# Values projected by three split products, a block table by one-hot products, and a gate weight split later

## The chip, the cores and the metric

One core of one Trainium2 chip runs the program. The metric is device time of one execution in microseconds (us): 2423.96 as the median of 3 runs (2423.73 to 2424.24).

The core has a matrix engine (PE, with its weight loads as PEld), a vector engine (DVE), a scalar engine (ACT), GpSimd (POOL) and a queue engine (SP). Each runs its own instructions strictly in order. An instruction may wait for a semaphore, and everything behind it on its engine then waits too.

## What is computed

One layer of a backbone over 2048 latent tokens and 256 context tokens of width 1024, in float32. This is what matters of the reference:

```
h   = rmsnorm(x) * (1 + scale) + shift                     # scale, shift from silu(c) @ w_mod
z, xbc, dt, q, k, v, g_out, gk = split(h @ w_in)           # one projection
xbc = silu(conv(xbc)); gates = log_sigmoid(gk @ gk_up + bias) / 16
two scans (SSD over xbc, dt; GLA over q, k, v, gates), both directions, context first
x   = x + gate * (concat(norm(ssd) * silu(z), norm(gla) * silu(g_out)) @ w_out)
ids, w = route(h2 @ w_router)                              # top 2 of 32 experts per token
slots: each (token, expert) pair gets a place in blocks of 128 rows, one expert to a block
x   = x + gate2 * sum_over_experts(w * mlp_e(h2));  out = rmsnorm(x)
```

`v` is the 512 columns of `w_in` from `O_V`; `z` and `g_out` are 512 columns each, from `O_Z` and `O_G`.

## The kernel before, in words

The stages run one after the other, each as a block of five instruction lists, with a barrier behind each: constants and modulation, projection, chunks, mixer, slots, experts, combine.

**Projection** (`projection`, lines 350 to 782). There are nine groups of 256 tokens, the context first (`it` 0), then eight of latents. `head` normalises a group (ACT squares, L494; POOL the root, L566; DVE scales, L686), PE transposes it (`turned`, L593) and DVE modulates it into `hT` (L695). `body` has on PE five pairs of feature products (L614, 128x256, plain float32), half a slab of the modulation (L267), the small columns (L628), and then per 128 tokens `s` the value product into `pz[s]` (L636, 8 products 128x512 in float32, each of which the trace shows as two instructions), with the transposes of the **next** group between and behind them. ACT takes each pair out of PSUM (L506, L512), then waits for DVE's convolution, applies Silu (L516), and only then squares the next group (`head(*after)`). So ACT's order is: fifth pair, Silu, next group's squares. In groups 5 to 7 one piece of the `z`/`g_out` weight is split in `w_hi` (ACT L547) and `w_lo` (DVE L776). A split is x = hi + lo, both in the reduced type fp32r.

**Chunks** (`chunks`). The product of `z` and `g_out` (L1060) is made of three fp32r products hi*hi, hi*lo, lo*hi per 128 rows `k`. `KA` = 3 pieces of the weight come split from the projection; pieces 3 to 5 are loaded there but split at the start of this stage, and pieces 6 and 7 are loaded (L871) as buffers come free, and split (ACT L939, DVE L1122) behind DVE's and ACT's first chunk work. PE waits per `k` for `w_lo_done`.

**Slots** (`slots`, lines 1821 to 2028). DVE works out each pair's slot in a chain of short instructions, each waiting for the one before (`then`), POOL clears a table `slot_tok` in DRAM, waits for the slots, and scatters 32 times 128 records of 16 words (token, weight) into it by indirect DMA (L1911). DVE meanwhile makes the block plan (L2008 to L2027).

**Experts** (`experts`). POOL loads the table (L2122), copies a block's indices (L2118) and gathers its rows (L2120). PE transposes them (`turn`, L2229), ACT and DVE split them (L2168, L2295) and the weights (L2163, L2289), PE multiplies (L2236).

## Time and profile before

| | us |
|---|---|
| median of 3 runs | 2423.96 |
| the profiled execution, whole | 2428.52 |
| its span in the profile | 2426.8 |
| modulation, until the first feature product | 0 to 53.9 |
| projection | 53.9 to 604.1 |
| chunks | 604.1 to 901 |
| mixer | 901 to 1321 |
| slots | 1321 to 1404.3 |
| experts | 1404.3 to about 2384 |
| combine | to 2426.8 |

PE is busy for 2164.6 us (89% of the span), DVE 1624.7 (67%), ACT 1137.1 (47%), POOL 529.8 (22%). To read it: times are us from the span's start, matmuls are pipelined, so a busy PE is not at its peak, and the profile also gives the clock that PE was granted, as a share of full speed (1.00 is 2.4 GHz, 0.50 is 1.2 GHz). Stages follow each other through barriers, so what one stage gains or loses shifts all behind it.

### The profile page before, as it was taken

How to read it: one execution, taken by the hardware profiler on the slowest of the kernel's cores; microseconds unless marked ns; L12 is line 12 of the kernel's file. 1: busy time of each engine (PE TensorE's matmuls, PEld its weight loads, DVE VectorE, ACT ScalarE, POOL GpSimd, SP SyncE). 2: the span in 40 equal slices, each digit the busy share in tenths (PEclk: the TensorE clock that was granted, in tenths of full speed). 3: DMA queues.
4: the chain of work that ended last, by engine and by line, in shares of the span. 5: the costliest groups of instructions: out<-in, count | busy, mean ns of one | idle time of the engine just before them, and what ended most of it. 6: DMA issues, size and time to landing. Idle time of an engine off the chain costs nothing. (4 is left out here: it accounts for less than half of the span.)

```text
span 2426.8 us, 36201 instructions
## 1 busy us (share of the span) xinstructions
PE 2164.6 (89%) x11697; PEld 1709.4 (70%) x11697; DVE 1624.7 (67%) x2071; ACT 1137.1 (47%) x1469; POOL 529.8 (22%) x536
## 2 busy tenths in 40 slices
PE   4999999998999987999996059999999999999980
PEld 2777777776777766888885048878788778778760
DVE  1333333433666667777773449999999999999983
ACT  0222222222555533333331047777777777777763
POOL 1000000000000001233322423333332333333332
PEclk7999999999999996899997579999999999999995
DMA  8123334322688745899874426478988779989957
GB/s 317 66 78 108 110 117 145 128 99 85 228 291 295 277 171 191 305 311 293 291 240 113 176 54 207 115 241 275 303 253 274 233 233 356 310 293 309 374 182 293
DMA packets 204877, 530.22 MB, mean 218 GB/s; under 512 B 14929, under 2 KB 46156, under 8 KB 198252
## 3 DMA queue, kind: packets, MB, share of 16 engines
q1 hardware_dynamic: 174904, 424.71, 48.8%
q0 software_dynamic: 26224, 91.57, 15.0%
q10 hardware_dynamic: 3651, 12.65, 1.4%
q8 instruction: 61, 1.00, 0.2%
q14 instruction: 37, 0.30, 0.0%
HBM read 398.64 MB, written 130.24 MB: 218 GB/s over the span
## 5 line engine op out<-in xcount | busy, mean ns | idle before, releaser
L2163 ACT ACTIVATE w_hi_e<-w_gates 128x2048 fp32r (+1 forms) x103 | 197.7, 1920 | 237.1 <-issue 104.1
L2289 DVE TENSOR_TENSOR w_lo_e<-w_gates,w_hi_e 128x2048 fp32r<-128x2048 f32 x103 | 236.4, 2296 | 33.2 <-ACT w_hi_e L2163 33.2
L2289 DVE TENSOR_TENSOR w_lo_e<-w_ups,w_hi_e 128x2048 fp32r<-128x2048 f32 x102 | 233.5, 2289 | 37.0 <-ACT w_hi_e L2163 37.0
L2289 DVE TENSOR_TENSOR w_lo_e<-w_downs,w_hi_e 128x2048 fp32r<-128x2048 f32 x100 | 228.4, 2284 | 0.0
L2163 ACT ACTIVATE w_hi_e<-w_ups 128x2048 fp32r (+1 forms) x102 | 195.2, 1914 | 24.8 <-PE pd_e L2236 22.4
L2163 ACT ACTIVATE w_hi_e<-w_downs 128x2048 fp32r x100 | 191.1, 1911 | 1.0
L614 PE MATMUL pf<-raws,w_in_sb 128*128 128x256 f32 x800 | 177.5, 385 | 1.1 <-DVE raws L695 1.1
L2236 PE MATMUL pg_e<-w_hi_e,x_hi_e 128*128 128x512 f32 x408 | 167.7, 411 | 7.2 <-DVE w_lo_e L2289 7.2
L614 PEld LDWEIGHTS pf<-raws,w_in_sb 128*128 128x128 f32 x800 | 154.1, 193 | 23.0 <-DVE raws L695 1.5
L2141 POOL DMA_INDIRECT x_mid<-yb_e,to_e x50 | 126.9, 2538 | 190.7 <-DVE yb_e L2333 188.6
L2236 PE MATMUL pg_e<-w_lo_e,x_hi_e 128*128 128x512 f32 x408 | 162.1, 397 | 0.0
L2236 PE MATMUL pd_e<-w_hi_e,h_hi_e 128*128 128x512 f32 x400 | 162.1, 405 | 0.0
L2236 PE MATMUL pg_e<-w_hi_e,x_lo_e 128*128 128x512 f32 x408 | 161.9, 397 | 0.0
L2236 PE MATMUL pd_e<-w_hi_e,h_lo_e 128*128 128x512 f32 x400 | 157.9, 395 | 0.0
L2236 PE MATMUL pu_e<-w_hi_e,x_hi_e 128*128 128x512 f32 x400 | 157.9, 395 | 0.0
L2236 PE MATMUL pu_e<-w_hi_e,x_lo_e 128*128 128x512 f32 x400 | 157.9, 395 | 0.0
L2236 PE MATMUL pu_e<-w_lo_e,x_hi_e 128*128 128x512 f32 x400 | 157.9, 395 | 0.0
L2236 PE MATMUL pd_e<-w_lo_e,h_hi_e 128*128 128x512 f32 x400 | 157.9, 395 | 0.0
L614 PE MATMUL pf<-hT,w_in_sb 128*128 128x256 f32 x640 | 143.8, 388 | 0.0
L2118 POOL COPY idx_e<-toks_e 128x1 int32 (+1 forms) x54 | 51.5, 954 | 400.7 <-DMA x_mid<-yb_e,to_e 335.9
L614 PEld LDWEIGHTS pf<-hT,w_in_sb 128*128 128x128 f32 x640 | 124.7, 195 | 17.7
L716 DVE TENSOR_SCALAR fm<-u_raw,cols 128x256 f32<-128x256 f32 x54 | 18.2, 411 | 176.2 <-ACT u_raw L506 176.2
(420 smaller groups left out, 4708.4 us busy)
## 6 DMA issues: line engine op xcount, KB each, us to landing
w_gates<-in_w_gate_dram SPq DMA_DIRECT2D x32, 2048.0 KB, 12.1
w_ups<-in_w_up_dram SPq DMA_DIRECT2D x32, 2048.0 KB
w_downs<-in_w_down_dram SPq DMA_DIRECT2D x32, 2048.0 KB
w_mod_half<-in_w_mod_dram SPq DMA_DIRECT2D x16, 1024.0 KB, 7.0
abc_m<-a_rows SPq DMA_DIRECT2D x16, 1024.0 KB, 4.9
recs<-tok_rec SPq DMA_DIRECT2D x15, 968.0 KB, 7.8
qk_rec<-qk SPq DMA_DIRECT2D x14, 1024.0 KB, 3.9
qk<-qk_rec SPq DMA_DIRECT2D x14, 1024.0 KB
```

The lines of the kernel that those rows point to most:

```text
L614: mm = pe.matmul(pf[n % 2][:, f, :], w[:, k, c0:c0 + P], h[:, k, :], start=(k == 0), stop=(k == KT - 1))
L716: i = dve.tensor_scalar(a, b, wt, cols[:, R_CB + f:R_CB + f + 1], ALU.mult, ALU.add)
L2118: pool.tensor_copy(idx[u][:, :], toks[:, bass.ds(b, 1), 0]).then_inc(idx_ready, 1)
L2141: pool.indirect_dma_start(out=x_mid, out_offset=bass.IndirectOffsetOnAxis(ap=to[u][:, 0:1], axis=0), in_=yb[:, :], in_offset=None, compute ...
L2163: act.activation(w_hi[:, s % 3:s % 3 + 1, :], raw(part, half, place), ACT.Copy).then_inc(hi_done, 1)
L2236: mm = pe.matmul(acc[:, :], a[:, k, :], w[:, s % 3, c], start=start and n == 0, stop=stop and n == 2)
L2289: dve.tensor_tensor(w_lo[:, s % 3:s % 3 + 1, :], raw(part, half, place), w_hi[:, s % 3:s % 3 + 1, :].bitcast(F32), ALU.subtract).then_inc( ...
```

## The change

Three edits go together.

**Values.** The `v` columns leave the big weight load (`W_LEN` falls from 1800 to 1288 columns). They are loaded apart, in pieces of 256 rows, at the start of the projection, and split once, in the context group, into `wv_hi` and `wv_lo`. Each 128 tokens of `hT` are split into `x_hi` (ACT, `high`) and `x_lo` (DVE, `low`), each with one buffer. The value product becomes 24 fp32r products (`values`). That of `s` = 0 now stands on PE **ahead of the fifth feature pair**, that of `s` = 1 between the two halves of the next group's transposes. `high` of `s` = 1 stands on ACT ahead of taking out the fifth pair.

**Gates' weight.** `KA` = 0: no piece is split in the projection, three are loaded at its end, and the chunk stage splits all eight.

**Block table.** POOL's clearing and 32 scatters, and the table's load in the experts, go. DVE makes, in four rounds of 8 tiles, a one-hot of each pair's place in its block (128x1024), a one-hot of its block (128x544), and this times token and weight; PE sums them by 32 float32 products 128x136 into PSUM, and DVE copies the table to SBUF at the end of its list.

```diff
@@ -51,7 +51,7 @@
 FF = 512
 EPS = 1e-6
 MAXB = 64
-KA = 3
+KA = 0
 BIG = 1e30
 
 
...
@@ -70,7 +70,7 @@
 T_DT = T_V + GW
 T_GF = T_DT + 2 * SH
 T_LEN = T_GF + 2 * GQK
-W_LEN = O_G - O_XBC
+W_LEN = O_V - O_XBC
 
 F_TILES = 6
 
...
-            slots(nc, A, C, route, slot_tok, weights, loaded, x_mid, h_rows)
-            experts(nc, A, C, route, slot_tok, weights, loaded, h_rows, x_mid)
+            toks = ctx.enter_context(nc.sbuf_tensor("toks", [P, TAB, 2], I32))
+            slots(nc, A, C, route, toks, weights, loaded, x_mid, h_rows)
+            experts(nc, A, C, route, toks, weights, loaded, h_rows, x_mid)
         combine(nc, A, x_mid, out)
 
 
...
             for k in range(KT):
-                sp.dma_start(w_in_sb[:, k, :], A["w_in"][0][k * P:(k + 1) * P, O_XBC:O_G]).then_inc(w_in_loaded, 16)
+                sp.dma_start(w_in_sb[:, k, :], A["w_in"][0][k * P:(k + 1) * P, O_XBC:O_V]).then_inc(w_in_loaded, 16)
...
-        w_raw, w_hi, w_lo = K["w_raw"], K["w_hi"][0], K["w_lo"][0]
-        SPLIT = LAT_GROUPS - KA
+        F32R = mybir.dt.float32r
+        w_raw = K["w_raw"]
+        wv_hi, wv_lo = sb("wv_hi", [P, KT, GW], F32R), sb("wv_lo", [P, KT, GW], F32R)
+        x_hi, x_lo = sb("x_hi", [P, KT, P], F32R), sb("x_lo", [P, KT, P], F32R)
+        wv_loaded = [sem(f"wv{b}_loaded") for b in range(3)]
+        wv_hi_done, wv_lo_done, x_hi_done, x_lo_done = (sem(n) for n in ("wv_hi_done", "wv_lo_done", "x_hi_done", "x_lo_done"))
+        PAIRS = KT // 2
...
+
+            def load_v(c):
+                if c >= 3:
+                    sp.wait_ge(wv_lo_done, c - 2)
+                for n in range(2):
+                    k = 2 * c + n
+                    sp.dma_start(w_raw[c % 3][:, n, :], A["w_in"][0][k * P:(k + 1) * P, O_V:O_G]).then_inc(wv_loaded[c % 3], 16)
+            for c in range(3):
+                load_v(c)
...
                 sp.dma_start(sel_dt[ONE:ONE + 1, SH * d:SH * (d + 1)], A[f"dt_bias_{n}"]).then_inc(small_loaded, 16)
 
             sp.dma_start(slab[:, :, :], w_mod_d[EARLY][0]).then_inc(slab_loaded, 16)
+            load_v(3)
...
-                if it == SPLIT - 1:
+                if it == LAT_GROUPS - 1:
+                    sp.wait_ge(wv_lo_done, PAIRS)
                     for k in range(3):
                         load_w(k)
-                if SPLIT <= it < LAT_GROUPS:
-                    sp.wait_ge(K["w_lo_done"], it - SPLIT + 1)
-                    load_w(it - SPLIT + 3)
...
+            def high(it, buf, s):
+                if s:
+                    act.wait_ge(tok_ps, it * 2 + 1)
+                else:
+                    act.wait_ge(ht_done, it * 4 + 4)
+                    if not it == 0:
+                        act.wait_ge(tok_ps, it * 2)
+                act.activation(x_hi[:, :, :], hT[buf][:, :, s * P:(s + 1) * P], ACT.Copy).then_inc(x_hi_done, 1)
+
...
 
+                high(it, buf, 0)
+                if is_ctx:
+                    for c in range(PAIRS):
+                        act.wait_ge(wv_loaded[c % 3], 32 * (c // 3 + 1))
+                        act.activation(wv_hi[:, 2 * c:2 * c + 2, :], w_raw[c % 3], ACT.Copy).then_inc(wv_hi_done, 1)
                 for n in range(5):
+                    if n == 4:
+                        high(it, buf, 1)
                     act.wait_ge(feat_ps, it * 5 + (n + 1))
...
-                if SPLIT <= it < LAT_GROUPS:
-                    k = it - SPLIT
-                    act.wait_ge(K["w_loaded"][k % 3], 32 * (k // 3 + 1))
-                    act.activation(w_hi[:, k, :, :], w_raw[k % 3][:, :, :], ACT.Copy).then_inc(K["w_hi_done"], 1)
...
+            def values(it, s, is_ctx):
+                if s == 0 and not is_ctx:
+                    pe.wait_ge(min_done, it * 4)
+                    pe.wait_ge(abs_done, it * 4)
+                if is_ctx:
+                    pe.wait_ge(wv_lo_done, PAIRS)
+                pe.wait_ge(x_lo_done, it * 2 + s + 1)
+                for k in range(KT):
+                    for j, (a, b) in enumerate(((x_hi, wv_hi), (x_hi, wv_lo), (x_lo, wv_hi))):
+                        mm = pe.matmul(pz[s][:, :], a[:, k, :], b[:, k, :], start=(k == 0 and j == 0), stop=(k == KT - 1 and j == 2))
+                mm.then_inc(tok_ps, 1)
...
                 for n in range(5):
+                    if n == 4:
+                        values(it, 0, is_ctx)
                     if n >= 2 or not is_ctx:
...
-                for s in range(2):
-                    if s == 0 and not is_ctx:
-
-                        pe.wait_ge(min_done, it * 4)
-                        pe.wait_ge(abs_done, it * 4)
-                    for k in range(KT):
-                        mm = pe.matmul(pz[s][:, :], h[:, k, s * P:(s + 1) * P], w[:, k, O_V - O_XBC:O_V - O_XBC + GW],
-                                       start=(k == 0), stop=(k == KT - 1))
-                    mm.then_inc(tok_ps, 1)
-                    if after is not None:
-                        turned(*after, range(2 * s, 2 * s + 2))
+                if after is not None:
+                    turned(*after, range(0, 2))
+                values(it, 1, is_ctx)
+                if after is not None:
+                    turned(*after, range(2, 4))
...
+            def low(it, buf, s):
+                dve.wait_ge(x_hi_done, it * 2 + s + 1)
+                dve.tensor_tensor(x_lo[:, :, :], hT[buf][:, :, s * P:(s + 1) * P], x_hi[:, :, :].bitcast(F32), ALU.subtract).then_inc(x_lo_done, 1)
...
             def body(it, use, buf, is_ctx, after):
 
+                low(it, buf, 0)
+                if is_ctx:
+                    for c in range(PAIRS):
+                        dve.wait_ge(wv_hi_done, c + 1)
+                        dve.tensor_tensor(wv_lo[:, 2 * c:2 * c + 2, :], w_raw[c % 3], wv_hi[:, 2 * c:2 * c + 2, :].bitcast(F32),
+                                          ALU.subtract).then_inc(wv_lo_done, 1)
...
                         i = dve.scalar_tensor_tensor(out=to, in0=fr, scalar=wt, in1=to, op0=ALU.mult, op1=ALU.add)
                     i.then_inc(conv_done if n == 4 else conv_step, 1)
 
+                low(it, buf, 1)
                 dve.wait_ge(small_ps, it + 1)
...
-                if SPLIT <= it < LAT_GROUPS:
-                    k = it - SPLIT
-                    dve.wait_ge(K["w_hi_done"], k + 1)
-                    dve.tensor_tensor(w_lo[:, k, :, :], w_raw[k % 3][:, :, :], w_hi[:, k, :, :].bitcast(F32), ALU.subtract).then_inc(K["w_lo_done"], 1)
...
-        w_his, w_los, w_raw = ([K[n][0], sb(n, [P, KT - KA, 2, SW], F32R)] for n in ("w_hi", "w_lo")), None, K["w_raw"]
-        w_his, w_los = w_his
+        w_his, w_los, w_raw = sb("w_hi", [P, KT, 2, SW], F32R), sb("w_lo", [P, KT, 2, SW], F32R), K["w_raw"]
         nega = K["nega"]
 
         def half(pair, k):
-            return pair[0][:, k, :, :] if k < KA else pair[1][:, k - KA, :, :]
+            return pair[:, k, :, :]
...
+            for k in range(NW, KT):
                 sp.wait_ge(w_lo_done, k - NW + 1)
                 load_w(k)
...
             features(CT)
-            weights(range(KA, KA + NW))
+            weights(range(NW))
             for i in range(TILES):
                 exponentials(i)
                 if i == 0:
-                    weights(range(KA + NW, KT))
+                    weights(range(NW, KT))
...
-        bnum = sb("bnum", [1, TAB])
+        bnum = sb("bnum", [P, TAB])
+        place, own = sb("place", [P, P]), sb("own", [P, TAB])
+        tok_f, val = sb("tok_f", [P, LT]), sb("val", [P, LT, 2])
+        pos_i, pos, blk_of = sb("pos_i", [P, LT, 2], I32), sb("pos", [P, LT, 2]), sb("blk_of", [P, LT, 2])
+        in_place = [sb(f"in_place{b}", [P, LT // 2, P]) for b in range(2)]
+        in_block, parts = [sb(f"in_block{b}", [P, LT // 2, TAB]) for b in range(2)], [sb(f"parts{b}", [P, LT // 2, 2, TAB]) for b in range(2)]
...
-        zero_i = sb("zero_i", [P, TAB * 16], I32)
-        slot_rec = sb("slot_rec", [P, LT, 2, 16], I32)
...
+        table = ps("table", [P, 2, TAB])
...
+            for c in range(4):
+                pe.wait_ge(parts_done, c + 1)
+                for i in range(LT // 2):
+                    mm = pe.matmul(table[:, :, :].rearrange("p a b -> p (a b)"), in_place[c % 2][:, i, :],
+                                   parts[c % 2][:, i, :, :].rearrange("p a b -> p (a b)"), start=(c + i == 0), stop=(c == 3 and i == LT // 2 - 1))
+                mm.then_inc(parts_used, 1)
...
-            pool.iota(slot_rec[:, :, :, :], pattern=[[P, LT], [0, 2], [0, 16]], base=0, channel_multiplier=1).then_inc(made, 1)
-            pool.iota(zero_i[:, :], pattern=[[0, TAB * 16]], base=SEQ, channel_multiplier=1).then_inc(made, 1)
...
-            pool.dma_start(slot_tok.rearrange("(b p) c -> p b c", p=P), zero_i[:, :].rearrange("p (b c) -> p b c", c=16)).then_inc(cleared, 16)
-            pool.wait_ge(cleared, 16)
-            pool.wait_ge(slot_done, 1)
-            for t in range(LT):
-                for j in range(2):
-                    pool.indirect_dma_start(out=slot_tok, out_offset=bass.IndirectOffsetOnAxis(ap=route["slot"][:, t, j:j + 1], axis=0),
-                                            in_=slot_rec[:, t, j, :], in_offset=None).then_inc(scattered, 16)
-            pool.wait_ge(scattered, 16 * 2 * LT)
             pool.wait_ge(spare_written, 32)
...
-            then(dve.tensor_copy(slot_rec[:, :, :, 1].bitcast(F32), route["gate"][:, :, :]))
...
             then(dve.tensor_copy(route["slot"][:, :, :], slot_f[:, :, :]))
-            dve.sem_inc(slot_done, 1)
+            then(dve.tensor_scalar(pos_i[:, :, :], route["slot"][:, :, :], P - 1, None, ALU.bitwise_and))
+            then(dve.tensor_copy(pos[:, :, :], pos_i[:, :, :]))
+            then(dve.tensor_tensor(blk_of[:, :, :], slot_f[:, :, :], pos[:, :, :], ALU.subtract))
+            then(dve.tensor_scalar(blk_of[:, :, :], blk_of[:, :, :], 1.0 / P, None, ALU.mult))
+            then(dve.tensor_tensor(val[:, :, :], tok_f[:, :].unsqueeze(2).to_broadcast([P, LT, 2]), pos[:, :, :], ALU.subtract))
+
+            H = LT // 2
+            for c in range(4):
+                j, t, b = c // 2, slice(H * (c % 2), H * (c % 2 + 1)), c % 2
+                if c >= 2:
+                    dve.wait_ge(parts_used, c - 1)
+                dve.tensor_tensor(in_place[b][:, :, :], place[:, :].unsqueeze(1).to_broadcast([P, H, P]),
+                                  pos[:, t, j].unsqueeze(2).to_broadcast([P, H, P]), ALU.is_equal)
+                then(dve.tensor_tensor(in_block[b][:, :, :], bnum[:, :].unsqueeze(1).to_broadcast([P, H, TAB]),
+                                       blk_of[:, t, j].unsqueeze(2).to_broadcast([P, H, TAB]), ALU.is_equal))
+                for n, of in enumerate((val, route["gate"])):
+                    op = dve.tensor_tensor(parts[b][:, :, n, :], in_block[b][:, :, :], of[:, t, j].unsqueeze(2).to_broadcast([P, H, TAB]), ALU.mult)
+                op.then_inc(parts_done, 1)
...
-            dve.sem_inc(plan_done, 1)
-
-
-def experts(nc, A, C, route, slot_tok, parts, w_loaded, h_rows, x_mid):
+            dve.wait_ge(parts_used, 4)
+            dve.tensor_tensor(toks[:, :, 0], table[:, 0, :], own[:, :], ALU.add).then_inc(plan_done, 1)
+            dve.tensor_copy(toks[:, :, 1].bitcast(F32), table[:, 1, :]).then_inc(plan_done, 1)
+            dve.wait_ge(plan_done, 2)
+
+
+def experts(nc, A, C, route, toks, parts, w_loaded, h_rows, x_mid):
...
-            pool.wait_ge(toks_loaded, 16)
             fetch(0, 0)
```

## Rows read from the trace of the kernel before

**Rows 1.** Projection: us, busy (count) by engine, PE clock, DMA share, GB/s

```profile
53.90:604.10 550.20, 528.78 (x2390) 384.89 (x2391) 208.89 (x497) 143.37 (x239) 14.63 (x32) 0.98 0.30 103
```

**Rows 2.** PE in order of time, groups 1 and 4

```profile
115.33 36.47 PE L614 MATMUL pf<-hT,w_in_sb 128*128 128x256 f32 x160
...
300.73 34.78 PE L614 MATMUL pf<-raws,w_in_sb 128*128 128x256 f32 x160
...
337.30 7.13 PE L636 MATMUL pz<-w_in_sb,raws 128*128 128x512 f32 x16
...
344.84 1.09 PE L593 MATMUL pt<-ident,xg 128*128 128x128 f32 x8 [0.41 <-DVE xg L686]
...
345.77 7.03 PE L636 MATMUL pz<-w_in_sb,raws 128*128 128x512 f32 x16
...
352.64 1.04 PE L593 MATMUL pt<-ident,xg 128*128 128x128 f32 x8
```

**Rows 3.** ACT and DVE in group 4, in order of time

```profile
335.55 0.60 ACT L512 ACTIVATE fm<-pf 128x512 f32<-128x512 f32 x1 [6.31 <-PE pf L614]
...
343.37 1.42 DVE L686 TENSOR_SCALAR xg<-xg,rstd 128x1024 f32<-128x1024 f32 x2 [5.45 <-POOL rstd L570]
```

**Rows 4.** Split products of the chunk stage, 21 steps apart

```profile
703.00 0.40 PE L1060 MATMUL pg_s<-w_zg_lo,x_hi_s 128*128 128x512 f32 x1
...
707.84 0.39 PE L1060 MATMUL pg_s<-w_lo_s,x_hi_s 128*128 128x512 f32 x1
```

**Rows 5.** Busy time by stretch of 1 us, columns as in rows 1

```profile
57.00:58.00 1.00, 1.00 (x4) 0.79 (x3) 0.00 (x0) 0.00 (x0) 0.00 (x0) 0.62 1.05 434
...
965.00:966.00 1.00, 0.39 (x8) 0.20 (x4) 1.00 (x3) 0.54 (x1) 0.00 (x0) 1.00 1.03 219
...
969.00:970.00 1.00, 0.00 (x0) 0.00 (x0) 1.00 (x3) 0.00 (x0) 0.00 (x0) 0.56 1.07 352
...
1429.00:1430.00 1.00, 1.00 (x4) 0.81 (x3) 1.00 (x1) 0.00 (x0) 0.00 (x0) 0.54 0.72 279
```

**Rows 6.** Start: GB/s in 40 slices of 0 to 70 us, then order of time

```profile
GB/s 0 179 403 385 372 390 383 389 390 400 399 390 390 389 386 419 416 424 424 416 424 420 416 428 416 286 30 11 249 352 0 70 407 122 0 0 0 0 0 0
...
53.93 16.38 PE L614 MATMUL pf<-raws,w_in_sb 128*128 128x256 f32 x66 [1.09 <-DVE raws L695]
```

**Rows 7.** Start of the chunk stage, in order of time

```profile
607.79 1.94 SPq L871 DMA_DIRECT2D raws<-in_w_in_dram  x4
...
611.91 1.06 ACT L939 ACTIVATE w_hi_s<-raws 128x1024 fp32r<-128x1024 f32 x1 [0.33 <-DMA raws<-in_w_in_dram]
...
615.03 1.23 DVE L1122 TENSOR_TENSOR w_lo_s<-raws,w_hi_s 128x1024 fp32r<-128x1024 f32 x1 [0.62 <-ACT w_hi_s L939]
...
616.31 0.50 PE L1060 MATMUL pz_s<-w_hi_s,x_hi_s 128*128 128x512 f32 x1 [0.87 <-DVE w_lo_s L1122]
```

**Rows 8.** Slots, in order of time

```profile
1333.17 0.69 DVE L1960 TENSOR_TENSOR eq_r<-eq_r,down_e_r 128x512 f32<-128x512 f32 x1
...
1355.92 0.18 DVE L2000 CAST slot<-slot_f_r 128x32 int32<-128x32 f32 x1
...
1364.33 0.14 DVE L2027 CAST plan<-eb_r 1x1 int32<-1x1 f32 x1
...
1398.35 0.96 POOL L1911 DMA_INDIRECT slot_tok<-slot_rec_r,slot  x1 [0.30 <-issue]
```

**Rows 9.** Start of the experts, in order of time

```profile
1404.32 3.76 PE L2218 MATMUL pd_e<-ident,mod 128*128 128x128 f32 x16 [53.45 <-PEq L107]
...
1411.38 4.49 DVE L2289 TENSOR_TENSOR w_lo_e<-w_gates,w_hi_e 128x2048 fp32r<-128x2048 f32 x2 [1.98 <-ACT w_hi_e L2163]
...
1416.76 1.03 POOL L2120 DMA_INDIRECT xg_e<-h_rows,idx_e  x1 [0.84 <-POOL idx_e L2118]
...
1421.23 1.94 PE L2229 MATMUL tx_e<-ident,xg_e 128*128 128x128 f32 x8 [13.16 <-DMA xg_e<-h_rows,idx_e]
...
1425.42 0.78 PE L2236 MATMUL pg_e<-w_hi_e,x_hi_e 128*128 128x512 f32 x1
```

More of the change, by code:

```diff
@@ L882, in _ @@
             load(CT)
-            for k in range(KA + NW, KT):
+            for k in range(NW, KT):
                 sp.wait_ge(w_lo_done, k - NW + 1)
@@ L1213, in _ @@
             features(CT)
-            weights(range(KA, KA + NW))
+            weights(range(NW))
             for n, src in enumerate((early, late)):
@@ L1222, in _ @@
                 if i == 0:
-                    weights(range(KA + NW, KT))
+                    weights(range(NW, KT))
                 if i == CT - 1:
@@ L1818, in load_part, with slots @@
                  A[("w_gate", "w_up", "w_down")[n]][0][e].rearrange("(k p) f -> p k f", p=P)).then_inc(w_loaded[n], 16)
-def slots(nc, A, C, route, slot_tok, weights, w_loaded, x_mid, h_rows):
+def slots(nc, A, C, route, toks, weights, w_loaded, x_mid, h_rows):
     logits, plan = route["logits"], route["plan"]
@@ L1897, in _ @@
                       allow_small_or_imprecise_dtypes=True).then_inc(made, 1)
-            pool.iota(slot_rec[:, :, :, :], pattern=[[P, LT], [0, 2], [0, 16]], base=0, channel_multiplier=1).then_inc(made, 1)
-            pool.iota(zero_i[:, :], pattern=[[0, TAB * 16]], base=SEQ, channel_multiplier=1).then_inc(made, 1)
+            pool.iota(place[:, :], pattern=[[1, P]], base=0, channel_multiplier=0,
+                      allow_small_or_imprecise_dtypes=True).then_inc(made, 1)
+            pool.iota(own[:, :], pattern=[[0, TAB]], base=SEQ, channel_multiplier=1,
+                      allow_small_or_imprecise_dtypes=True).then_inc(made, 1)
+            pool.iota(tok_f[:, :], pattern=[[P, LT]], base=-SEQ, channel_multiplier=1,
+                      allow_small_or_imprecise_dtypes=True).then_inc(made, 1)
             pool.memset(spare[:, :], 0.0).then_inc(made, 1)
-            pool.wait_ge(made, 7)
+            pool.wait_ge(made, 8)
             pool.dma_start(x_mid[SEQ:SEQ + P, :], spare[:, :]).then_inc(spare_written, 16)
             pool.dma_start(h_rows[SEQ:SEQ + P, :], spare[:, :]).then_inc(spare_written, 16)
-            pool.dma_start(slot_tok.rearrange("(b p) c -> p b c", p=P), zero_i[:, :].rearrange("p (b c) -> p b c", c=16)).then_inc(cleared, 16)
-            pool.wait_ge(cleared, 16)
-            pool.wait_ge(slot_done, 1)
-            for t in range(LT):
-                for j in range(2):
-                    pool.indirect_dma_start(out=slot_tok, out_offset=bass.IndirectOffsetOnAxis(ap=route["slot"][:, t, j:j + 1], axis=0),
-                                            in_=slot_rec[:, t, j, :], in_offset=None).then_inc(scattered, 16)
-            pool.wait_ge(scattered, 16 * 2 * LT)
             pool.wait_ge(spare_written, 32)
@@ L1927, in over_e @@
                 return x.unsqueeze(2).to_broadcast([P, LT, NE])
-            dve.wait_ge(made, 7)
+            dve.wait_ge(made, 8)
             dve.wait_ge(bias_loaded, 16)
@@ L2008, in _ @@
             then(dve.tensor_scalar(last[:, :], bend[0:1, NE - 1:NE], -1.0, None, ALU.add))
-            then(dve.tensor_tensor(blk[:, :], bnum[:, :], last[:, :].to_broadcast([1, TAB]), ALU.min))
+            then(dve.tensor_tensor(blk[:, :], bnum[0:1, :], last[:, :].to_broadcast([1, TAB]), ALU.min))
             then(dve.tensor_tensor(past[:, :, :], by_block(blk[:, :]), by_expert(bend[0:1, :]), ALU.is_ge))
@@ L2022, in _ @@
             then(dve.tensor_copy(plan[:, PL_LOAD:PL_LOAD + TAB], due[:, :]))
-            then(dve.tensor_tensor(npf[:, :], bnum[:, 0:MAXB].rearrange("p (a b) -> p a b", b=2)[:, :, 0],
+            then(dve.tensor_tensor(npf[:, :], bnum[0:1, 0:MAXB].rearrange("p (a b) -> p a b", b=2)[:, :, 0],
                                    bend[0:1, NE - 1:NE].to_broadcast([1, MAXB // 2]), ALU.is_lt))
@@ L2070, in experts @@
         to_ready = sem("to_ready")
-        (pool_held, sync_held, act_held, toks_loaded, idx_ready, gate_ps, gate_done, hi_done, lo_done, used, xt_ps,
+        (pool_held, sync_held, act_held, idx_ready, gate_ps, gate_done, hi_done, lo_done, used, xt_ps,
          xhi_done, xlo_done, silu_done, h_done, ht_ps, hhi_done, hlo_done, y_copied, y_free, y_done, stored) = (
-            sem(n) for n in ("pool_held", "sync_held", "act_held", "toks_loaded", "idx_ready", "gate_spread",
+            sem(n) for n in ("pool_held", "sync_held", "act_held", "idx_ready", "gate_spread",
                              "gate_done", "w_hi_done", "w_lo_done", "piece_used", "x_transposed", "x_hi_done", "x_lo_done",
@@ L2130, in _ @@
             pool.wait_ge(gate_done, 2)
[L2131 removed]
+            pool.tensor_copy(to[0][:, :], toks[:, 0, :]).then_inc(to_ready, 1)
             def body(r, u):
```

13 lines of the change are left out of this document (3 added, 10 removed).

## The prediction

> **What bounds the kernel now.** I read the clock and span first (one core, no disturbed die to set aside), then the 40 slices and the busy time by stretch, then PE's instructions in order of time in the stages that the diff touches, with what ended each idle time. In the projection PE is busy for 528.8 of 550.2 us at clock 0.98 [rows 1]: it is bound by PE, and what counts there is the time of PE's instructions plus the waits between them. The one wait that matters here is small: in group 4 PE waits 0.41 us at 344.84 for the next group's normalised rows, and no longer, because the value product of the first 128 tokens (from 337.30) covers the rest of that chain [rows 2]. The chunk stage opens with PE waiting for the last two weight pieces [rows 7]. In the slots PE hardly runs: the end is set by POOL, which issues the 32 scatters until 1399.3, while DVE is done at 1364.5 [rows 8]. The experts open with a wait for the table and the gather [rows 9]. So the change shortens one serial stage, and edits three places where PE sets the time.
>
> **The start.** The weight load loses 512 of 1800 columns in 1024 rows, 2.1 MB. The queues move about 420 GB/s without a break until some 45 us (26 slices of 1.75), when this load, the last of them, is in; DVE's first step waits for it, and PE's first feature product follows at 53.93 [rows 6]. 2.1 MB / 420 GB/s = 5.0: **-5.0**. The value weight (2.1 MB) comes behind it on the same queue; SP issues it ahead of its constants, and the last quarter after one split is done, about 10 us later. Its splits (four of 1.06 on ACT, four of 1.23 on DVE, the durations of rows 7) must be ready only when PE has done four feature pairs, some 28 us in (five take 34.8 [rows 2]). That covers it. Without the cover each late us would be a us.
>
> **The groups.** A value product now takes 6.87 us (345.77 to 352.64 [rows 2]). 21 steps of split products last 4.84, so one is 0.2305, and 24 are 5.5 [rows 4]: 1.35 less. The splits of the tokens (two of 1.06 on ACT and two of 1.23 on DVE per group) lie beside PE's work: the first beside the first pairs, the second beside the fifth pair, as PE needs it only after the next transposes. I cost them at nothing.
>
> What costs is the place. The fifth pair is taken out at 335.55, DVE scales the next group at 343.37, and PE transposes at 344.84 [rows 2, 3]: 9.3 us of ACT's Silu and squares, POOL's root and DVE's scaling, serial by ACT's order. Behind the fifth pair PE has 1.75 us of work (335.55 to 337.30), and before, the first value product filled the rest. Now this stands **ahead** of the fifth pair. It delays that pair, and so the whole chain, by 5.5, and leaves 9.3 - 1.75 = 7.5 us with nothing on PE. Queued behind this wait are the second value product, half a slab, the gates and the back transposes. The chain to the transposes grows by 5.5, the second product gives back 1.35: +4.15 in each of the eight groups that have a next one, **+33.2**. The ninth has none and gains twice 1.35: **-2.7**.
>
> **The clock in these stalls.** This no row of the projection shows, so I bound it from elsewhere. In the mixer PE goes idle in the stretch 965 to 966 at clock 1.00, and the clock falls to 0.50 within 969 to 970 [rows 5]. After the start, dense products begin at 53.93 at 0.50, and the clock rises about 57.8 (0.62 in the stretch 57 to 58) [rows 5, 6]; in the experts they begin at 1425.42 and it rises about 1429.9 [rows 5, 9]. So a stall of 7.5 ends at half clock, and then some 4.2 us pass at half speed, a loss of 2.1, and eight transposes take 1.94 in place of 1.09 [rows 2, 9]: 2.9 per stall, **+23.2** for eight. The ends are 0 and, if a whole second product stays at half clock, 5.5 + 0.85 = 6.4 each, +51. I take 2.9, since it rests on dense products after a stall, as here.
>
> A rule of the Trainium skill speaks against the change: "TensorE: Matmul & The Clock Gate", section "Why this matters for your kernels", warns that a long wait between bursts of matmuls drops the engine to half clock, and that the next burst starts cold. The mixer's rows agree; whether the projection's stalls do so no row shows. By the rule all eight stalls pay.
>
> Another page would make the products cheaper: "FP8 and Floating Point Precision", section "TensorE Precision Notes", has true float32 as four passes. Three split products of one pass each would then be 5.15 per 128 tokens where the row gives 5.5, an estimate by which the sum would be 6 lower. The row decides.
>
> **The chunk stage.** Before, PE's product waited for pieces 6 and 7 only; its last wait ended at 616.31 and three products followed [rows 7]. Now pieces 0 to 2 are split where 3 to 5 were, and five remain. Piece 3 takes the place of 6 (loaded at 611.9), piece 4 that of 7, piece 5 follows one split later. The load of piece 6 needs the buffer of 3, free at 614.4, and that of 7 the buffer of 4, free at 616.25. A load took 4.1 (queued at 607.79, used at 611.91), then ACT takes 1.06 and DVE 1.23 [rows 7]: the last piece is ready at 616.25 + 4.1 + 1.06 + 1.23 = 622.6, 6.4 later than before: **+6.4**, since PE is busy almost without a break behind it. Ends: 3.7 (three more splits on DVE, were the loads free) and 9 (a load of 6.7). What leaves groups 5 to 7 lay beside PE and saves nothing.
>
> **Slots and experts.** From the slots (1356.1) on, DVE has new work ahead of the plan: five short steps of about 0.22, then four rounds of one 128x1024 (1.2, as in rows 7) and three 128x544 (0.7 each, as 128x512 in rows 8), 3.3 each. PE has 16 instructions of 136 columns per round; at half clock 16 of 128 columns took 3.76 [rows 9], so it keeps pace a little behind, and DVE waits perhaps 0.8 for its buffers. With 0.4 for the copies: 1.1 + 13.2 + 0.8 + 0.4 = 15.5, so DVE ends at 1364.5 + 15.5 = 1380.0. The plan covers PE's last round. From POOL's last scatter (1399.3) to the first expert instruction (1404.32) it took 5.0, with the landing [rows 8, 9]; without it I take 3.0 (ends 0 and 5): the experts start at 1383.0, **-21.3**.
>
> In the experts the table's load goes. POOL gathered at 1416.76, rows were there at 1421.23, PE multiplied from 1425.42, 21.1 after the stage's start [rows 9]. Now the gather can start some 2.8 in, rows are there at 7.3, but DVE's two splits end only at 11.5 (1411.38 + 4.49), and then the tokens' splits and transposes run to about 14: **-7.1**. The ends are -5 and -9.7 (the whole load). The next late thing there is DVE.
>
> **Sum.** -5.0 + 33.2 - 2.7 + 23.2 + 6.4 - 21.3 - 7.1 = +26.7. The profiled execution took 2428.52 (span 2426.8) and would take 2455.2; the median of the runs is 4.6 lower, so the forecast is 2424.0 + 26.7 = 2450.7, said as 2451.
>
> **Rivals.**
> A. The clock holds: the new stalls stay too short for it to fall. For it: PE works densely for some 55 us between them, and 0.98 is the mean now. Against: rows 5. It gives 2424.0 + 26.7 - 23.2 = 2427.5, no change.
> B. Faster: the place is the projection's clock. Now four groups pay 36.5 in place of 34.8 for their five pairs [rows 2], a fall at their head. If split products keep the clock up all through, the stalls cost no clock and these four falls (4 x 1.7 = 6.8) go: 2420.7. It counts as faster from 1.6 us more on, and the experts' start may give 2.6 more (-9.7): 2418.1. Against it: a longer idle time in each group.
> C. Slower still: each second value product runs wholly at half clock: +51 in place of +23.2, 2478.5. For it: in the stretch from 1421.23 transposes alone did not raise the clock [rows 5, 9]. Against: both dense bursts got it back in about 4 us.
> D. The chain does not hang on the fifth pair, and the stall is short. I see no way: ACT's list has the squares behind it. It would give 2424.0 - 5.0 - 9 x 2.7 + 6.4 - 28.4 = 2372.7.
>
> **Chances.** Forecast 0.75, A 0.10, B 0.05, C 0.08, D 0.02. A measurement of this kernel can tell about 0.2%, 4.8 us, from no change. Faster is B and D: 0.07. Same is A and a low tail of the forecast: 0.13. Slower: 0.80. The range takes in A and the forecast with its bounds, and leaves out B, C and D: 2426 to 2464.
>
> **What would show it.** In the profile after: the first feature product near 49; between the small columns and the next transposes a wait of 7 to 8 us for DVE's scaling, eight times; clock 0.50 behind each, so a mean of about 0.93 in the projection; groups 64 to 68 us long in place of about 60 to 62; in the chunk stage the last wait for a split ending some 18.5 us after PE's first instruction there in place of 12.2 (604.1 to 616.3); slots 62 us long; the first expert product 14 after the stage's start. I am wrong if the stall is short, if the clock stays at 1.00 behind it, or if DVE's one-hot rounds take much over 3.3 each.

## The result: 14.4 us slower, and the profile after

| | before | after |
|---|---|---|
| median of the runs, us | 2423.85 (4 runs, 2421.23 to 2424.24) | 2438.24 (4 runs, 2437.35 to 2439.21) |
| ratio to before, 95% interval | | 1.0062 (1.0044 to 1.0079) |
| profiled execution: time, span, us | 2428.52, 2426.8 | 2439.13, 2437.4 |

The change costs 14.4 us by the medians and 10.6 by the two profiled executions; that of before lies 4.7 above its median, that of after 0.9. The terms below come from the traces, so they add up to 10.6.

From the page of after: the span, PE's busy time, and the granted clock in the 40 slices.

```profile
span 2437.4 us, 36666 instructions
...
PE 2161.3 (89%) x11905; PEld 1756.5 (72%) x11905; DVE 1663.6 (68%) x2115; ACT 1158.3 (48%) x1491; POOL 494.3 (20%) x503
...
PEclk8999999999899997799999679999999999999995
```

By stage (us, then busy time and count of PE, PEld, DVE, ACT and POOL, then PE's clock, DMA share and GB/s): the projection from its first feature product, the chunk stage with the mixer, the slots, and the experts.

```profile
48.95:639.54 590.59, 513.73 (x2534) 421.85 (x2535) 231.59 (x516) 162.28 (x258) 14.62 (x32) 0.94 0.28 96
...
639.54:1365.07 725.53, 682.56 (x4932) 564.63 (x4932) 479.72 (x843) 287.80 (x677) 125.48 (x177) 0.93 0.74 250
...
1365.07:1423.20 58.13, 14.80 (x70) 11.48 (x71) 48.91 (x107) 1.91 (x2) 2.92 (x10) 0.62 0.64 235
...
1423.20:2390.00 966.80, 930.40 (x4256) 749.21 (x4256) 874.33 (x611) 683.44 (x511) 328.04 (x209) 0.98 0.77 252
```

In the projection PE is busy for 513.7 of 590.6 us at clock 0.94; in [rows 1] it was 528.8 of 550.2 at 0.98. It has less to do and more to wait for. The slots take 58.1 us in place of 83.2 (1321.08 to 1404.32). Put against the stages' starts before (53.93, 604.10, 1321.08, 1404.32):

| term | forecast | measured, from the starts of the stages and groups |
|---|---|---|
| start | -5.0 | -5.0 (first feature product 53.93, now 48.95) |
| eight groups: waits and products | +33.2 | +32.9 (waits 58.3 in place of 2.8; 16 value products 1.41 shorter each) |
| eight groups: clock | +23.2 | +10.2 (the rest of 532.1 in place of 489.0) |
| last group | -2.7 | -2.7 (58.53 in place of 61.21) |
| chunk stage and mixer | +6.4 | +8.5 (725.5 in place of 717.0) |
| slots | -21.3 | -25.1 |
| experts | -7.1 | -8.3 |
| sum | +26.7 | +10.5 |

The wait, in order of time (start, us, engine, line, operation; in brackets the idle time before it and what ended it), in group 6:

```profile
488.15 0.60 ACT L538 ACTIVATE fm<-pf 128x512 f32<-128x512 f32 x1 [5.85 <-PE pf L650]
...
488.77 1.28 ACT L542 ACT_TABLE_LOAD   x1
...
490.06 1.48 ACT L542 ACTIVATE fm<-fm 128x1536 f32<-128x1536 f32 x1
...
491.45 0.61 ACT L504 ACTIVATE soft<-xg 128x512 f32<-128x512 f32 x1
...
495.21 0.71 POOL L592 TENSOR_TENSOR rstd<-rstd,mhalf 128x2 f32<-128x2 f32 x1
...
495.96 1.42 DVE L716 TENSOR_SCALAR xg<-xg,rstd 128x1024 f32<-128x1024 f32 x2 [5.43 <-POOL rstd L592]
...
497.43 1.97 PE L615 MATMUL pt<-ident,xg 128*128 128x128 f32 x8 [7.46 <-DVE xg L716]
...
505.14 1.03 PE L615 MATMUL pt<-ident,xg 128*128 128x128 f32 x8
```

PE is done with the fifth pair and the small columns at 489.97 and then stands still for 7.46 us. The rows to read are ACT's: its eviction of the fifth pair (taking it out of PSUM), which PE ended at 488.1, a table load of 1.28 ahead of the Silu, the Silu over 1536 columns of the features, the first of the four squares, then POOL's power and DVE's scaling. Between the eviction's start and PE's transposes lie 9.28 us, of which the table load is 1.28. The same chain stood in [rows 2, 3] behind a wait of 0.41.

Behind the wait the clock is at half. In group 2, PE's transposes and the first product at full speed:

```profile
231.50 1.97 PE L615 MATMUL pt<-ident,xg 128*128 128x128 f32 x8 [7.46 <-DVE xg L716]
...
237.44 0.39 PE L631 MATMUL pz<-wv_lo,x_hi 128*128 128x512 f32 x1
```

and three stretches of 1 us of the same group, columns as above:

```profile
232.00:233.00 1.00, 1.00 (x6) 1.00 (x5) 0.28 (x1) 0.00 (x0) 0.00 (x0) 0.50 1.15 346
...
236.00:237.00 1.00, 1.00 (x4) 0.81 (x3) 0.00 (x0) 0.00 (x0) 0.00 (x0) 0.50 0.00 0
...
238.00:239.00 1.00, 1.00 (x6) 0.82 (x5) 0.00 (x0) 0.00 (x0) 0.00 (x0) 1.00 0.00 0
```

Eight transposes take 1.97 in place of 1.04, products come 0.43 apart until 237.44 and 0.23 apart from there.

### The profile page after: what moved, and what is told of

Its sections match the earlier page's. It is cut to its first block and busy times, and to the rows that moved or that the text cites. A ratio compares the mean times of both kernels' runs of the same rounds, so it can differ in the third digit from the quotient of the medians.

```text
span 2437.4 us, 36666 instructions
## 1 busy us (share of the span) xinstructions
PE 2161.3 (89%) x11905; PEld 1756.5 (72%) x11905; DVE 1663.6 (68%) x2115; ACT 1158.3 (48%) x1491; POOL 494.3 (20%) x503
## 5 line engine op out<-in xcount | busy, mean ns | idle before, releaser
L2346 DVE TENSOR_TENSOR w_lo_e<-w_gates,w_hi_e 128x2048 fp32r<-128x2048 f32 x103 | 236.3, 2295 | 33.9 <-ACT w_hi_e L2220 33.9
L2177 POOL COPY idx_e<-toks 128x1 int32 (+1 forms) x54 | 53.4, 989 | 445.7 <-DMA x_mid<-yb_e,to_e 338.6
```

The lines of the kernel that those rows point to most:

```text
L2177: pool.tensor_copy(idx[u][:, :], toks[:, bass.ds(b, 1), 0]).then_inc(idx_ready, 1)
L2346: dve.tensor_tensor(w_lo[:, s % 3:s % 3 + 1, :], raw(part, half, place), w_hi[:, s % 3:s % 3 + 1, :].bitcast(F32), ALU.subtract).then_inc( ...
```

## Experiments

Ten kernels, each timed beside the kernel before on the same chip (its median there 2421.9 to 2423.6). The eight transposes of the next group's first 128 tokens and those of its second have the second value product between them. From the start of the first eight to that of the second (the transposes' distance below) it is 6.43 at full clock, in after 8.81, 7.96, 9.15, 8.15, 9.27, 8.23, 7.71 and 8.20, 8.44 on the mean.

**The place.** The first value product goes back behind the fifth pair. The second token split goes with it, on ACT behind the squares and on DVE behind the scaling (not shown in the cut).

```diff
                 for n in range(5):
-                    if n == 4:
-                        values(it, 0, is_ctx)
...
                 mm.then_inc(small_ps, 1)
+                values(it, 0, is_ctx)
                 if after is not None:
                     turned(*after, range(0, 2))
```

> The changed kernel with the first 128 tokens' value product behind the fifth feature pair and the small columns again; the second token split follows on ACT and DVE behind the squares and the scaling. Theory (the place makes the stall): the fifth pair is no longer delayed, its chain of 9.3 us is covered by 1.75 + 5.5, so a wait of about 2.0 us for DVE's scaling is left in place of 7.46, and about 0.25 us for the second split: 5.2 less in each of eight groups, -42. If waits of 2 us do not let the clock fall, the clock's loss goes too (-15), and the falls at the groups' heads may come back (up to +7): 2438.2 - 42 - 8 to -15 = 2381 to 2388; 2396 if the clock still falls. Rival (the split products and their splits themselves cost the time, wherever they stand): about 2438, the wait only moved.

Measured: 2385.04 (2384.46 to 2387.33), 0.9844 (0.9828 to 0.9860) of before.

```profile
152.74 1.06 ACT L516 ACTIVATE x_hi<-hT 128x1024 fp32r<-128x1024 f32 x1 [1.27 <-PE pz L630]
...
154.48 1.09 PE L614 MATMUL pt<-ident,xg 128*128 128x128 f32 x8 [1.78 <-DVE xg L714]
...
161.19 1.04 PE L614 MATMUL pt<-ident,xg 128*128 128x128 f32 x8
...
390.60 1.09 PE L614 MATMUL pt<-ident,xg 128*128 128x128 f32 x8 [1.79 <-DVE xg L714]
...
398.92 1.04 PE L614 MATMUL pt<-ident,xg 128*128 128x128 f32 x8
```

The first row is the second token split on ACT. The wait is 1.78 or 1.79 in seven groups (0.37 in the first). In five of the seven the clock holds behind it (1.09, and 6.71 between the transposes). In two, the last two rows and the group of 510.27, the transposes still take 1.09, but the clock falls just behind them and their distance is 8.32. No group behind the first has a slow head here. So 53 us of after are the place of one product with its split, and with it in the old place the whole change makes the kernel 38 us faster.

**The filler, too long.** Products whose result nobody uses, in the wait, to keep PE busy without shortening the chain.

```diff
                 mm.then_inc(small_ps, 1)
                 if after is not None:
+                    for i in range(33):
+                        pe.matmul(pz[1][:, 0:GRP], w[:, 0, 0:P], h[:, i % KT, :], start=True, stop=True)
                     turned(*after, range(0, 2))
```

> The changed kernel with 33 products of 128x256, whose result nobody uses, behind the small columns in the groups that have a next one: 33 x 0.218 = 7.2 us of PE's work in the wait of 7.46 for DVE's scaling. The chain to the transposes stays as long, so the wait itself is neither shorter nor longer. Theory (the clock falls in the wait, and what follows pays for it): clock 1.00 behind it, transposes 1.04 in place of 1.97, all split products 0.23 apart: eight times 1.2 to 2.8, about -15, 2423; -10 if falls at the groups' heads come back. Rival (the clock's falls have nothing to do with the wait): 2438. If the products outlast the wait, up to +0.2 each group.

Measured: 2480.21 (2478.47 to 2480.98), 1.0235 (1.0218 to 1.0252).

```profile
92.52 14.51 PE L668 MATMUL pz<-raws,w_in_sb 128*128 128x256 f32 x66
...
106.87 1.04 PE L615 MATMUL pt<-ident,xg 128*128 128x128 f32 x8
```

I had taken 0.218 us, the time of one traced instruction, for a product. In true float32 a product is two of them (66 here for 33), so the filler took 14.4 and outlasted the wait by some 7.0 on the mean of the groups: 2480 where I expected 2423. What the run does show is that the clock holds: 1.04, and 6.38 to the second pair.

**The filler, right size:** 16 products in place of 33.

> The run with the filled wait had its filler too long: the trace counts a product of 128x256 in true float32 as two instructions, so 33 of them took 14.4 us (92.52 to 106.87) and outlasted the wait by 7.05 in each of eight groups, 56.4 in all; its time less that is 2480.2 - 56.4 = 2423.8. Here 16 of them, 16 x 0.436 = 7.0 us, in the wait of 7.46; the result is used by nobody. Theory (the clock falls in the wait and what follows pays about 2.0 in each group, by the first and the second transposes 8.44 apart on the mean in place of 6.43): 2438.2 - 16 = 2422, or up to 2427 if falls at the groups' heads come back. Rival (the clock's falls are not the wait's): 2438.

Measured: 2423.40 (2422.10 to 2425.58, 10 runs), 1.0001 (0.9992 to 1.0011).

```profile
156.10 7.17 PE L668 MATMUL pz<-hT,w_in_sb 128*128 128x256 f32 x32
...
163.63 1.09 PE L615 MATMUL pt<-ident,xg 128*128 128x128 f32 x8 [0.36 <-DVE xg L718]
...
170.05 1.03 PE L615 MATMUL pt<-ident,xg 128*128 128x128 f32 x8
```

PE gets its rows no sooner than in after, and the kernel is 14.8 us faster: that is the price of the clock, with what differs by chance between two traces. In the trace the eight groups are 518.2 long, 13.8 less than in after. Against the 16.0 of eight times 2.0 stand two things: three groups (the second, fifth and eighth) are 1.65 longer than the others again, a fall at their head, where after had one; and the first four pairs of the stage ran at full clock here (27.89 in place of 29.88), which has nothing to do with the waits and flatters the filler by 2.0.

**The chain.** The product stays where the change put it; the squares go ahead of the fifth pair's eviction on ACT, and DVE scales ahead of the copy of the small columns.

```diff
                 for n in range(5):
                     if n == 4:
+                        if after is not None:
+                            head(*after)
                         high(it, buf, 1)
...
                 act.activation(fm[:, 0:6, :], fm[:, 0:6, :], ACT.Silu).then_inc(silu_done, 1)
-                if after is not None:
-                    head(*after)
...
                 low(it, buf, 1)
+                if after is not None:
+                    scaled(*after)
                 dve.wait_ge(small_ps, it + 1)
```

> The changed kernel, product order kept, with the next group's squares on ACT ahead of the fifth pair's eviction and DVE's scaling ahead of the copy of the small columns. Theory (the transposes hang on the fifth pair by ACT's order alone, not by data): the rows are scaled before PE has done the fifth pair, the wait of 7.46 is gone, and with it the clock's fall: -59.7 and -10 to -15, 2363 to 2369. Rival (something else is late next: the load of the rows, POOL's root, DVE's convolution ahead of the scaling): a wait of 2 to 5 us is left, 2380 to 2410.

Measured: 2364.72 (2360.61 to 2368.05), 0.9759 (0.9740 to 0.9778).

```profile
137.40 0.62 ACT L504 ACTIVATE soft<-xg 128x512 f32<-128x512 f32 x1
...
141.18 0.77 POOL L592 TENSOR_TENSOR rstd<-rstd,mhalf 128x2 f32<-128x2 f32 x1
...
144.63 1.41 DVE L716 TENSOR_SCALAR xg<-xg,rstd 128x1024 f32<-128x1024 f32 x2
...
151.06 1.09 PE L615 MATMUL pt<-ident,xg 128*128 128x128 f32 x8
...
157.49 1.04 PE L615 MATMUL pt<-ident,xg 128*128 128x128 f32 x8
```

ACT squares while PE multiplies the first value product, the rows are scaled at 146.0, 5 us before PE wants them, and PE goes on without a wait. The eight groups take 458.8: 59.4 less than with the filler, close to the 58.3 of the traced waits, and 73.3 less than after. So the chain hung on the fifth pair by the order of ACT's and DVE's lists alone, and not by data.

**The same order in the kernel before.**

> The kernel before with the order of the run with early squares: the next group's squares on ACT ahead of the fifth pair's eviction, DVE's scaling ahead of the copy of the small columns; nothing else. Theory (this order pays only where nothing covers the chain): the wait of 0.41 in each of eight groups goes, -3.3: 2420. Rival (the order is worth the 73 us that it gave in the changed kernel, or a part of it, by something else than the wait): 2400 or less. Beside the run with the table alone this prices the split products in a good order: 2364.7 against 2393.0 - 3.3.

Measured: 2421.04 (2420.27 to 2422.83), 0.9993 (0.9984 to 1.0003). Within the measurement of nothing, as -3.3 would be. In its trace the seven waits of 0.4 (the first group had none) are gone, 2.8 us in all, and five groups have a fall at their head where before had four. The order is worth 73 us where the chain lies bare, and nearly nothing where one product covers it.

**The block table alone:** slots and experts of after, everything ahead of them as before.

> The kernel before with the block table's part of the change alone (slots and experts), the projection and chunk stages as before. By the traces, the slots are 25.1 and the experts 8.3 shorter: 2423.9 - 33.4 = 2390.5. The terms of the forecast gave -21.3 - 7.1: 2395.5. Rival (what the slots give is taken back in the experts by the weight loads, which wait for the same queues): 2400 and more.

Measured: 2392.97 (2390.70 to 2393.41), 0.9871 (0.9854 to 0.9887), 30 us; in its trace the slots take 58.0 (1319.24 to 1377.29), as in after, and PE's last expert product is 944.2 behind the experts' start (952.2 before). Both gains stand, and the rival falls. The two expectations lie 2.5 on either side of the time, so the runs don't tell them apart; the trace does.

**All eight pieces of the gates' weight split in the chunk stage,** and nothing else.

> The kernel before with all eight pieces of the gates' weight split in the chunk stage, and nothing else of the change. By the forecast's term +6.4: 2429.5; by the traces (the chunk stage and the mixer together were 8.55 longer in the changed kernel) 2431.7. Rival (what leaves the projection's last groups gives it back): 2423 to 2426.

Measured: 2431.24 (2428.32 to 2432.99), 1.0033 (1.0022 to 1.0044): +7.6. The first row is the product behind piece 6, the second that behind piece 7, the third a stretch:

```profile
617.94 0.79 PE L1045 MATMUL pz_s<-w_hi_s,x_hi_s 128*128 128x512 f32 x1 [1.23 <-DVE w_lo_s L1107]
...
620.20 0.79 PE L1045 MATMUL pz_s<-w_hi_s,x_hi_s 128*128 128x512 f32 x1 [0.61 <-DVE w_lo_s L1107]
...
617.00:627.00 10.00, 8.45 (x40) 6.89 (x40) 2.11 (x2) 1.25 (x3) 0.00 (x0) 0.51 0.02 8
```

The stage and the mixer together took 724.9 (601.97 to 1326.9), 7.9 more than before, and the projection 2.1 less. That isn't the splits' going: the trace has two slow heads where before has four, and the unchanged projection of the table alone has five. In the stretch of the third row PE runs at half clock.

**A short wait.** The run with early squares and 3 unused products (1.3 us) in the wait of 1.40 between the back transposes.

```diff
                         if q >= 2:
+                            if q == 2:
+                                for i in range(3):
+                                    pe.matmul(pf[0][:, 0, :], w[:, 0, 0:P], h[:, i, :], start=True, stop=True)
                             pe.wait_ge(back_done, it * 4 + (q - 1))
```

> The run with early squares, and 3 products of 128x256 in true float32 (3 x 0.436 = 1.3 us, result used by nobody) in the wait of 1.40 us for DVE's copy between the back transposes, the longest wait left in a group. In that run three of nine groups still began with a fall of the clock, about 1.6 us each. Theory (that wait brings these falls): they go, 2364.7 - 5 = 2360. Rival (they have another cause): no change, 2364 to 2366.

Measured: 2356.85 (2354.99 to 2358.36), 0.9726 (0.9710 to 0.9742).

```profile
160.94 1.46 PE L693 MATMUL pf<-hT,w_in_sb 128*128 128x256 f32 x6
```

Seven groups are 56.7 long, none has a fall. (The expectation counted three falls; the first was the slow clock of the start, which is there in both, 58.7 and 58.5. Two falls of 1.5 are gone.) Of the 7.9 us between the medians the projection shows 3.2, the chunk stage and mixer 2.7. The first is the falls. The second lies in the mixer: with early squares the clock is at 0.50 from 872 to 902 there, in this trace it is back at 1.00 from 879 to 881. The edit touches nothing of that stage; whether it is more than a difference between two executions, no run shows.

**The same without a filler:** the last two sets of back transposes go to the feature products' two banks, and the next group's first pairs wait for the copies.

```diff
+        back = [t[:, :] for t in pt] + [t[:, :, :].rearrange("p a b -> p (a b)") for t in pf]
...
+                    if n < 2 and not is_ctx:
+                        pe.wait_ge(back_done, it * 4 - 1 + n)
...
-                            pe.wait_ge(back_done, it * 4 + (q - 1))
+                            pass
```

> The run with early squares, with no filler: the third and fourth set of back transposes go to the two PSUM banks of the feature products, which are free there, so PE needn't wait for DVE's copy of the first. Theory (the short wait costs itself and brings the clock's falls at the groups' heads): the wait of 1.40 goes in nine groups, -12.6, and the falls too, -5 to -8: the run with the gap filled (2356.9) less nine times the filler's 1.3 us or a little less, since the next group's first feature pair may wait for the third copy up to 0.3 us: 2345 to 2348. Rival (the falls come back without the filler, as PE is idle no less elsewhere): 2350 to 2353. Rival (DVE's copies, not the banks, hold PE): 2360 or more.

Measured: 2356.02 (2352.03 to 2356.96), 0.9725 (0.9712 to 0.9738).

```profile
159.51 0.93 PE L701 MATMUL pf<-ident,fm 128*128 128x128 f32 x7
...
162.22 8.01 PE L653 MATMUL pf<-raws,w_in_sb 128*128 128x256 f32 x36 [0.99 <-DVE qk L805]
```

A miss: I expected 2345 to 2348, and 2356 is in neither rival's range. The wait moved. PE transposes without a break and then stands 0.99 us ahead of the next first pair, for DVE's third copy; groups are 56.2 long, 0.5 shorter than with the filler, and not 1.3. DVE's copies set this end as soon as the banks don't. No head has a fall. With the filled gap this is the fastest kernel of the case, 2.75% below before.

**A wait of half the length:** after with 8 unused products.

> The changed kernel with 8 of the unused products ahead of the transposes: 3.5 us of the wait of 7.46 filled, 4.0 left. The runs show the clock kept behind waits of 0.4 and 1.8 us and lost behind 7.46. If a wait of 4.0 keeps it, the time is that of the filled wait, 2423; if it loses it in all eight groups as 7.46 does, 2438; in between, a fall in some groups or shorter stretches at half clock. By what the trace of the mixer shows (half clock within 4 to 5 us of the last product) I expect falls in the stretch behind it, 2430 to 2438.

Measured: 2437.44 (2433.95 to 2439.44), 1.0059 (1.0043 to 1.0074).

```profile
157.44 3.72 PE L668 MATMUL pz<-hT,w_in_sb 128*128 128x256 f32 x16
...
164.98 1.57 PE L615 MATMUL pt<-ident,xg 128*128 128x128 f32 x8 [3.81 <-DVE xg L718]
...
168.48 0.57 PE L631 MATMUL pz<-wv_hi,x_lo 128*128 128x512 f32 x1
...
168.89 0.39 PE L631 MATMUL pz<-wv_hi,x_hi 128*128 128x512 f32 x1
```

3.8 us of waiting cost in sum about as much clock as 7.46, though in another way. Seven groups have this wait. In four of them the transposes are half slow (1.51 to 1.57), some six products follow at half clock, and the group has a fall at its head as well; in the other three all eight transposes are slow (1.97) and the head is not (groups of 67.5 and 65.6 in turn). By the transposes' distance the seven lose 10.5, where after lost 16.0 in eight, and the heads 6.8 in place of 1.7. The first group's wait is 2.39, and behind it the clock holds (1.10).

## Why the prediction was right, step by step

The direction and the range held; the size was 12 too high (26.7 against 14.4, or 16 against the traces).

- **Start, last group: as said.** 48.95, and 2.7.
- **The wait: as said.** The step from "ahead of the fifth pair" to "9.3 - 1.75 = 7.5 on PE" gave 7.46 in seven of eight groups (6.04 in the first), and the runs show it from two sides: with the product behind the pair 1.78 is left, with the squares ahead of it nothing. Rival D (the chain doesn't hang on the pair) was wrong for this kernel, but the reason I gave against it, ACT's list, was also the cure.
- **The clock: the right mechanism, two mis-sized terms.** I charged 2.9 per wait from the rows of the start and of the experts' start. It cost 2.0 (16.0 in all, by the transposes' distance). The transposes lost the 0.9 I gave them; the dense time at half clock behind them was 1.2 to 4.5 us in place of 4.2, and in four groups of eight about 2. So the rows of the start and of the experts were the far end and not the middle; that they come out of a longer idle time may be why, but no run shows it. The second term I had only in rival B: the falls at the groups' heads. After has one in its eight long groups, where before has four (36.2 to 36.5 in place of 34.8), which gives 4.7 back. So B's number came true in part inside the forecast; its reason, that split products keep the clock up, is not shown, since the same products have two to four slow heads in other runs (early squares, both fillers, the wait of 3.8), and the number differs between traces of one projection (four in before, five with the table alone). So this part of the term may belong to the two traces compared as much as to the change. 16.0 less 4.7 is 11.3 against 10.2 in the table; the last 1.1 I can't place. It is 14.8 by the filled wait, which has three such falls of its own. A and C are out: the clock did not hold (0.50 in the rows), and no second product ran wholly at half clock.
- **The rule of the clock.** The Trainium skill, "TensorE: Matmul & The Clock Gate", section "Why this matters for your kernels", says that a long wait between bursts leaves the next burst cold. This case agrees for waits of 7.46 (eight transposes 1.97 each time) and in three of seven groups for 3.8; in the other four the transposes began at full clock and ended at half. Behind 0.4 and 2.39 nothing was slow, but behind 1.79 the clock fell in two groups of seven, 1.1 us into the burst.
- **The chunk stage: the place right, the clock forgotten.** I said the last wait would end 18.5 behind PE's first instruction; it is 17.95 (639.54 to 657.49). But I took PE as fast as before from there:

```profile
649.51 1.06 ACT L975 ACTIVATE w_hi_s<-raws 128x1024 fp32r<-128x1024 f32 x1 [1.09 <-DMA raws<-in_w_in_dram]
...
649.89 0.50 PE L1096 MATMUL pz_s<-w_hi_s,x_hi_s 128*128 128x512 f32 x1 [1.91 <-DVE w_lo_s L1158]
...
655.51 0.79 PE L1096 MATMUL pz_s<-w_hi_s,x_hi_s 128*128 128x512 f32 x1 [0.70 <-DVE w_lo_s L1158]
...
657.49 0.80 PE L1096 MATMUL pz_s<-w_hi_s,x_hi_s 128*128 128x512 f32 x1 [0.33 <-DVE w_lo_s L1158]
...
650.00:660.00 10.00, 8.26 (x19) 4.99 (x19) 4.90 (x4) 3.93 (x6) 0.00 (x0) 0.52 0.34 107
```

The first row is ACT's split of piece 4, the next three are products behind waits. There are four such waits, of 0.33 to 1.91, with three to six products between them, and PE runs those 10 us at 0.52: the product behind its last wait takes 0.80, where before it took 0.50 [rows 7]. Set against the same instructions of before, PE is 5.8 late at this last wait and 8.6 late at 663.6, shortly before the clock is back. So the waits cost 5.8 where I had 6.4, and the half clock behind them 2.8 where I had nothing. The run with the late split alone has the same slow stretch and 7.6.

- **The slots and the experts: 5 too little.** From the cast of the slots to the first wide product:

```profile
1398.99 0.18 DVE L2040 CAST slot<-slot_f_r 128x32 int32<-128x32 f32 x1
...
1400.31 1.22 DVE L2052 TENSOR_TENSOR in_place_r<-place_r,pos_r 128x1024 f32<-128x1024 f32 x1
...
1413.99 0.13 DVE L2065 TENSOR_SCALAR last_r<-bend_r 1x1 f32<-1x1 f32 x1
...
1421.97 0.22 DVE L2087 COPY toks<-table_r 128x68 f32<-128x68 f32 x1
...
1423.20 3.75 PE L2275 MATMUL pd_e<-ident,mod 128*128 128x128 f32 x16 [6.95 <-PEq L107]
...
1437.09 0.77 PE L2293 MATMUL pg_e<-w_hi_e,x_hi_e 128*128 128x512 f32 x1
```

The four one-hot rounds take 3.2 to 4.2 with their wait for PE, 13.7 in all against 14.0 said. Of the 3.8 that I missed, 2.0 are the step from DVE's last copy to PE's first expert instruction: 1.0, where I took 3.0 from a stage end that had a DMA's landing in it. 0.9 are ahead of the new work: DVE's part up to the cast takes 33.9 in place of 34.8. The first wide product comes 13.9 behind the stage's start, as said; the other 1.1 of the experts are behind it, in 930.1 us in place of 931.2, which is run-to-run size.
- **The products' price.** 24 in a row are 0.2275 apart, 5.5 each 128 tokens, as the row said. The estimate of 5.15 from the Trainium skill ("FP8 and Floating Point Precision", section "TensorE Precision Notes") was too low here.

## What to carry to other kernels

When work is moved ahead of an instruction, follow what hangs on that instruction through every engine's list, not through the data: here 5.5 us of useful work in the wrong place opened a wait of 7.46 in each group, and one reordering on ACT and DVE closed it and turned +14 into -58. Price such a wait twice, once for its length and once for the clock behind it, and take the second from several such waits: behind the same 7.46 it was 1.3 to 2.8 us, 2.0 on the mean. A wait that a filler of known length closes without shortening the chain measures the clock's part by itself.

## What the runs showed of the hardware that I had not expected

- The fall of the clock is not fixed by the wait. Behind the same 7.46, the products ran slow for between 1.2 and 4.5 us from group to group; behind 3.8, the transposes themselves began fast and ended slow in four groups of seven. Waits of 0.4 and one of 2.39 cost nothing of this; behind 1.79 the clock held in five groups and fell in two, where the second value product took 7.35 in place of 5.75.
- Groups with no wait over 1.40 still had a fall of 1.4 to 1.7 us at some heads (three with the filled wait, two with early squares), and none once the 1.40 was filled or cut to 0.99, in one trace each. Every other trace has one to five slow heads, save that with the product behind the pair, which has none there and two behind its waits of 1.79. So even this short wait seems tied to them; how, and why after has only one, stays open.
- In the chunk stage PE ran 10 us at 0.52 around four waits, none over 1.91, with three to six products between them, while one wait of 1.79 between long stretches of products mostly cost none. What makes the difference, no run takes apart.
- A 128x256 product in true float32 is two traced instructions, 0.436 together, and a split product of 128x512 is one, 0.23.
